# A fused mixer and mixture-of-experts block: x squared on two engines, z in column groups, other release points for loads, expert 0 picked apart, last weights by columns

## What is computed

```python
h = rms_norm(x, norm_mix)
(cb, cc, cx, aq, ak, av, gq, gk, gv, gr, gz) = split(h @ w_in)     # gz: 16 columns, z
y_conv = short_conv(cb, cc, cx, conv_w, conv_b)
y_attn = moba_attention(rms_norm(aq), rms_norm(ak), av, rel_bias_table)
y_gla  = gla(gq, gk, gv, gr, gz, w_gla_alpha, ...)                 # uses gz @ w_gla_alpha
merged = sum_n sigmoid(h @ w_merge_gate[n]) * (y_n @ w_branch[n])
x  = x + merged @ w_out
h2 = rms_norm(x, norm_ffn)
x  = x + hier_moe(h2, ...)   # group by argmax of 4, then the top 2 of its 8 experts, weights from softmax;
                             # y = sum over the two chosen e: w * ((silu(h2 @ w_g[e]) * (h2 @ w_u[e])) @ w_d[e])
```

## Time and profile before

| | before |
|---|---|
| time of the runs, median (lowest to highest) | 712.26 us (711.34 to 715.14), 3 runs |
| profiled execution: time, span | 712.9 us, 711.1 us |
| PE busy | 587.2 us, 83% |
| DVE, ACT, POOL busy | 302.8, 189.7, 29.6 us |
| DMA moved | 247.73 MB, mean 348 GB/s |
| granted TensorE clock, mean | 0.894 |

### The profile page before, as it was taken

One profiled execution on the slowest core, in us unless ns is written; L12 is line 12 of the kernel. 1 busy time (PEld: TensorE's weight loads), 2 busy tenths in 40 slices (PEclk: granted clock), 3 DMA queues, 4 the chain that ended last, 5 costly groups with the idle time before them and its releaser, 6 DMA issues.

```text
span 711.1 us, 15452 instructions
## 1 busy us (share of the span) xinstructions
PE 587.2 (83%) x6636; PEld 410.9 (58%) x6636; DVE 302.8 (43%) x626; ACT 189.7 (27%) x332; POOL 29.6 (4%) x56
## 2 busy tenths in 40 slices
PE   8999999999999999996875767776678656887584
PEld 5787899999999885553432333333334333443342
DVE  6475976985474945442222222122312222111412
ACT  4493355473535434110111001010011100110111
POOL 8003000000000020000000000000000000000000
PEclk9999999999999999998798788797877988687969
DMA  8995546536579699999999999999999999999993
GB/s 253 349 328 187 163 137 203 175 121 213 175 274 420 234 395 369 427 425 428 425 427 425 426 429 427 426 427 427 425 425 428 427 427 427 424 426 427 423 417 146
DMA packets 39619, 247.73 MB, mean 348 GB/s; under 512 B 4360, under 2 KB 6496, under 8 KB 25472
## 3 DMA queue, kind: packets, MB, share of 16 engines
q1 hardware_dynamic: 38096, 245.44, 85.6%
q0 software_dynamic: 912, 1.25, 1.0%
q10 hardware_dynamic: 544, 0.06, 0.1%
HBM read 245.67 MB, written 1.06 MB: 347 GB/s over the span
## 4 chain that ended last, share of the span: by engine, by line
PE 50%; DMA 44%; SPq 1%; another core or an unknown queue 1%; DVE 1%; issue 1%; ACT 0%; ACTq 0%; DVEq 0%
DMA wide<-in_w_expert_up 38%; PE ps L1366 8%; PE ps L1029 6%; PE ps L1030 6%; PE ps L1031 6%; DMA wide<-in_w_expert_down 3%; PE ps L1401 3%; PE ps L1002 3%; PE ps L1004 3%; PE ps L1003 3%; PE ps L1325 2%; DMA ring<-in_w_in 2%; PE ps L1413 1%; PE ps L1381 1%; SPq L526 1%
## 5 line engine op out<-in xcount | busy, mean ns | idle before, releaser
L1366 PE MATMUL ps<-wide,xe 128*32 128x256 f32 x2048 | 162.1, 470 | 109.3 <-DMA wide<-in_w_expert_up 109.3
L1366 PEld LDWEIGHTS ps<-wide,xe 128*32 128x32 f32 x2048 | 75.9, 131 | 176.9 <-issue 132.1
L1882 DVE TENSOR_TENSOR xe<-ps,g_ffn 128x256 f32<-128x256 f32 x32 | 13.6, 425 | 258.4 <-PE ps L1334 258.4
L1486 DVE TENSOR_TENSOR ring_lo<-ring,w_hi 128x1024 fp32r<-128x1024 f32 x76 | 92.0, 1228 | 46.2 <-ACT w_hi L721 45.7
L721 ACT ACTIVATE w_hi<-ring 128x1024 fp32r<-128x1024 f32 x76 | 79.0, 1058 | 58.8 <-PE ps L1031 35.3
L1029 PE MATMUL ps<-hT_hi,w_hi 128*128 128x256 f32 x320 | 89.4, 279 | 0.2 <-DVE hT_lo L1498 0.2
L1030 PE MATMUL ps<-hT_lo,w_hi 128*128 128x256 f32 x320 | 88.4, 276 | 0.0
L1031 PE MATMUL ps<-hT_hi,ring_lo 128*128 128x256 f32 x320 | 88.4, 276 | 0.0
L925 ACT ACTIVATE he<-ps 128x128 f32<-128x128 f32 x32 | 8.9, 278 | 207.7 <-PE ps L1381 204.7
L1401 PE MATMUL ps<-wide,he 128*32 128x256 f32 x1024 | 62.5, 382 | 1.9 <-DMA wide<-in_w_expert_down 1.8
L1029 PEld LDWEIGHTS ps<-hT_hi,w_hi 128*128 128x128 f32 x320 | 60.1, 188 | 0.7 <-issue 0.7
(11 more groups left out here) (276 smaller groups left out, 785.9 us busy)
## 6 DMA issues: line engine op xcount, KB each, us to landing
wide<-in_w_expert_gate SPq DMA_DIRECT2D x27, 2048.0 KB, 45.6
wide<-in_w_expert_up SPq DMA_DIRECT2D x27, 2048.0 KB, 48.2
wide<-in_w_expert_down SPq DMA_DIRECT2D x27, 2048.0 KB, 41.1
ring<-in_w_in SPq DMA_DIRECT2D x8, 2048.0 KB, 16.1
ring<-in_w_merge_gate SPq DMA_DIRECT2D x6, 2048.0 KB, 9.6
wide<-in_w_expert_gate SPq DMA_DIRECT2D x10, 1024.0 KB, 13.2
wide<-in_w_expert_up SPq DMA_DIRECT2D x10, 1024.0 KB, 10.6
wide<-in_w_expert_down SPq DMA_DIRECT2D x9, 1024.0 KB, 11.8
```

The lines of the kernel that those rows point to most:

```text
L1366: ins = t_.matmul(ps[q * WIN:(q + 1) * WIN, b, 0:QW], xe[b][:, k % 2, k // 2, :], w, start=(k == 0), stop=(k == KD - 1))
L1486: v.tensor_tensor(piece(ring_lo, g, c), piece(ring, g, c), by_row(out_hi[g == 19][c]).bitcast(F32), ALU.subtract).then_inc(wpre_lo, 1)
```

## The change

1. Front. Tile 1 of x is squared and summed by ACT; roots and reciprocals are taken for each tile by itself; DVE multiplies in four halves (features k 0 to 3 of both tiles, then 4 to 7), and PE turns each half when it is there. 14 warm-up matmuls for 20. Group 1 no longer waits for the small loads; w_z is loaded by ACT's queue; w_al is loaded four times, by SP behind group 1 (after two new memsets of POOL); POOL's 15 small loads wait for group 1.
2. z. 16 fp32 matmuls without hi and lo, slice k into the column group k mod 4, so that four parts of z lie in 128 partitions; w_al's four copies sum them in the next matmul.
3. w_out. New events after the halves of out_half and after the matmuls of out_quarter(1, q) that read ring_lo, which come first now. They release 12 and 14, 16, and 17.
4. Routing. in_group(0) and best_two(0) stand before x1_add(1, 2). Expert 0's own places come from six small matmuls on a mask `first`; the 14 `spots`, slots, table and pass count follow behind rows_in(0, 0). Seeds are single quarters in other places. SP issues units 22 to 25 before it reads the number of passes.
5. Tail. The last unit comes in column pieces of 512, 256 and 256; down, ACT's copy and combine of expert 31 run piece by piece in fp32 without y_lo, DVE makes all final copies, and SP stores six blocks.

The diff, cut to its core:

```diff
-N_WARM = 20
+N_AHEAD = 4
+N_WARM = 14
+LAST = (slice(0, 2 * QW), slice(2 * QW, 3 * QW), slice(3 * QW, D))
+LAST_Q = ((0, 1), (2,), (3,))
@@ SP
-                elif n < 16:
+                elif n in (12, 14):
+                    sp.wait_ge(chunk_done, chunks_before[NPRE - 2] + 1)
+                elif n in (13, 15):
                     sp.wait_ge(proj_done, first_bank[NPRE - 2] + 2)
-                elif n in (16, 18):
+                elif n == 16:
+                    sp.wait_ge(chunk_done, chunks_before[NPRE - 2] + 2)
+                elif n == 18:
                     sp.wait_ge(proj_done, first_bank[NPRE - 2] + 4)
+                elif n == 17:
+                    sp.wait_ge(chunk_done, chunks_before[NPRE - 2] + 3)
...
+                    if g == 1:
+                        sp.wait_ge(sbd_zero, 1)
+                        for q in range(NQ):
+                            sp.dma_start(w_al[WIN * q:WIN * q + 16, :], w_gla_alpha[0]).then_inc(alpha_in, 16)
...
-                    sp.wait_ge(early_in, 16 * N_EARLY)
-                    sp.dma_start(w_z[:, :, :], w_in_v[:, :, 4608:4624]).then_inc(wz_in, 16)
...
+            for n in range(RING, RING + N_AHEAD):
+                next_load(n, 0)
             sp.wait_ge(route_ready, 1)
@@ POOL
+            g.memset(w_z[:, :, 16:WIN], 0.0)
+            g.memset(w_al[:, :], 0.0).then_inc(sbd_zero, 1)
...
+            pool.wait_ge(landed[1], 16)
             for dst, src in smalls:
@@ ACT
-            act.wait_ge(ms_ready, 2)
-            s_.activation(stat[:, 2:4], stat[:, 0:2], ACT.Sqrt).then_inc(rms_ready, 1)
+            act.wait_ge(x_in[1], 16)
+            s_.activation(xn[:, 1, :], x_tok[:, 1, :], ACT.Square, accum_out=stat[:, 1:2]).then_inc(x_sq, 1)
+            for tt in range(TT):
+                act.wait_ge(ms_ready, tt + 1)
+                s_.activation(stat[:, 2 + tt:3 + tt], stat[:, 6 + tt:7 + tt], ACT.Sqrt).then_inc(rms_ready, 1)
...
+            def y_last(p):
...
+                for i, qs in enumerate(LAST_Q):
...
+                    s_.activation(y_end[rows_i, :], ps[rows_i, 0, 0:QW], ACT.Copy,
+                                  scale=w_slot[rows_i, ...]).then_inc(y_last_ready, 1)
@@ PE, z
-                t_.matmul(o, w_z_hi[:, k, :], hT_hi[:, k, :], start=(k == 0), stop=False)
-                t_.matmul(o, w_z_hi[:, k, :], hT_lo[:, k, :], start=False, stop=False)
-                ins = t_.matmul(o, w_z_lo[:, k, :], hT_hi[:, k, :], start=False, stop=(k == KD - 1))
+            for j in range(KD // NQ):
+                for h in (hT_hi, hT_lo):
+                    for q in range(NQ):
+                        ins = t_.matmul(ps[WIN * q:WIN * (q + 1), 4, 0:T], w_z[:, k, :], h[:, k, :].bitcast(F32), ...)
@@ PE, w_out and routing
+                if tt and ks[0] == 0:
+                    for k in range(KD):
+                        ins = t_.matmul(o, merged_hi[:, k, rows], wl[k], start=(k == 0), stop=False)
+                    ins.then_inc(chunk_done, 1)
...
-            out_quarter(1, 1, range(0, 4))
+            out_quarter(1, 1, range(0, 2))
...
-            out_quarter(1, 1, range(4, 6))
+            out_quarter(1, 1, range(2, 6))
...
+            seed(0, 0)
             route(1, range(6, KD), 6)
-            seed(0, 0)
+            seed(0, 2)
+            seed(1, 0)
+            seed(1, 2)
             seed(0, 1)
+            seed(0, 3)
...
+            for k in range(TOPK):
+                first_spot(tri_bf[:, :], 0, k, 0, start=(k == 0), stop=False)
+                first_spot(ones_bf[:, :], 0, k, 1, start=False, stop=False)
+                ins = first_spot(tri_bf[:, :], 1, k, 1, start=False, stop=(k == TOPK - 1))
             ins.then_inc(pos_mm, 1)
+            seed(1, 1)
...
             pick_rows(0, 0)
+            seed(1, 3).then_inc(seeded, 1)
             turn_rows(0, 0)
-            seed(1, 1).then_inc(seeded, 1)
+            all_spots()
@@ PE, tail
+            def down_last(p):
...
+                    for j in range(2):
+                        for q in qs:
+                            ins = t_.matmul(ps[q * WIN:(q + 1) * WIN, 0, 0:QW], he[:, 2 + j, :], ...)
...
+                    if i:
+                        combine_last(p, i - 1)
+                combine_last(p, 2)
@@ DVE
-            norm_stats(x_tok, [xn[:, tt, :] for tt in range(TT)], ms_ready)
-            norm_apply(x_tok, xn, rms_ready, xn_ready)
+            norm_stats(0)
+            norm_stats(1)
+            norm_apply(0, range(0, 4))
+            norm_apply(1, range(0, 4))
+            norm_apply(0, range(4, KD))
+            norm_apply(1, range(4, KD))
...
             group_of(0)
+            in_group(0)
+            best_two(0)
             x1_add(1, 2)
             square_sum(1, 2)
             mean_square(1)
-            in_group(0)
             scale_out(1)
-            best_two(0)
             group_of(1)
...
+            rows_in(0, 0)
+            slots()
             dve.wait_ge(table_ready, 1)
             choose(0, 1)
-            rows_in(0, 0)
```

More of the change, by code:

```diff
@@ L184, in hybrid_block @@
         le = place("le", [P, TT, NE], F32)
+        first = place("first", [P, TT, TOPK], BF16)
         eh = place("eh", [P, TT, TOPK, NE], BF16)
@@ L240, in hybrid_block @@
         scr = here("scr", [P, 2, C], F32)
+        w_z = place("w_z", [P, KD, WIN], F32, at=scr_at)
         la, e_pos, e_neg, e_rest = (qTz[:, 2 * i:2 * i + 2, :] for i in range(4))
@@ L582, in _ @@
                         load_unit(n)
[L583 to L594, removed]
+                    for n in range(RING, RING + N_AHEAD):
+                        next_load(n, UNITS * p)
+                for n in range(RING + N_AHEAD, UNITS):
+                    next_load(n, UNITS * p)
+            for i, cols_i in enumerate(LAST):
+                for tt in range(TT):
+                    sp.wait_ge(fin_ready, 2 * i + tt + 1)
+                    sp.dma_start(out[0, tt * P:(tt + 1) * P, cols_i], fin[tt][:, cols_i]).then_inc(stored, 16)
+            sp.wait_ge(stored, 16 * TT * len(LAST))
         @block.gpsimd
@@ L777, in _ @@
                 s_.activation(scr[:, tt, :], bank(4 if tt == 0 else 7), ACT.Square).then_inc(o_sq, 1)
-            act.wait_ge(o_ms, 1)
-            s_.activation(stat[:, 16:24], stat[:, 8:16], ACT.Sqrt).then_inc(o_rms, 1)
+            act.wait_ge(head_ms, 1)
+            s_.activation(stat[:, 16:24], stat[:, 8:16], ACT.Sqrt).then_inc(head_rms, 1)
             act.wait_ge(small_in, 16 * N_SMALL)
@@ L787, in _ @@
             high_pre(5, (1, 2, 3))
-            act.wait_ge(qk_ms, 1)
-            s_.activation(qkr[:, :, :, :], qkm[:, :, :, :], ACT.Sqrt).then_inc(qk_rms, 1)
+            act.wait_ge(head_ms, 2)
+            s_.activation(qkr[:, :, :, :], qkm[:, :, :, :], ACT.Sqrt).then_inc(head_rms, 1)
             high_pre(6, (0, 1, 2))
@@ L909, in _ @@
             rows_copy(0, 0)
+            act.wait_ge(slot_ready, 1)
+            s_.activation(flat(tab[:, :, :]), ps[:, 3, 2 * NE:4 * NE], ACT.Copy).then_inc(table_ready, 1)
             passes = act.alloc_register("passes_act")
@@ L954, in _ @@
                 y_high(p, NE - 2)
-                y_high(p, NE - 1)
-            for tt in range(TT):
-                act.wait_ge(combined, turns * (4 * NE) + 8)
-                s_.activation(fin[tt][:, 0:C].rearrange("p (q n) -> p q n", q=2), ps[:, 4:6, QW * tt:QW * (tt + 1)], ACT.Copy).then_inc(fin_act, 1)
+                y_last(p)
         @block.tensor
@@ L1230, in out_quarter @@
                     wh = out_hi[1][c][:, QW * (k % 4):QW * (k % 4 + 1)]
[L1231 to L1233 removed]
+                    t_.matmul(o, merged_hi[:, k, rows], wh, start=(tt == 0 and k == 0), stop=False)
+                    if tt == 0:
+                        t_.matmul(o, merged_hi[:, k, rows], wl[k], start=False, stop=False)
                     ins = t_.matmul(o, merged_lo[:, k, rows], wh, start=False, stop=(k == KD - 1))
@@ L1243, in turn_x1, with seed @@
                 ins.then_inc(x1_turned, 1)
-            def seed(tt, half):
-                for q in (2 * half, 2 * half + 1):
-                    ins = t_.matmul(bank(4 + q, 2)[:, tt, :], ident[:, :], x_tok[:, tt, QW * q:QW * (q + 1)],
-                                    start=(tt == 0), stop=False, skip_group_check=True)
-                return ins
+            def seed(tt, q):
+                return t_.matmul(bank(4 + q, 2)[:, tt, :], ident[:, :], x_tok[:, tt, QW * q:QW * (q + 1)],
+                                 start=(tt == 0), stop=False, skip_group_check=True)
             def route(tt, ks, copied):
```

253 lines of the change are left out of this document (148 added, 105 removed).

## The result

| | before | after |
|---|---|---|
| time of the runs, median (lowest to highest) | 712.57 us (711.34 to 715.14), 4 runs | 722.14 us (719.00 to 723.03), 4 runs |
| profiled execution: time, span | 712.9, 711.1 us | 721.93, 720.1 us |
| PE, DVE, ACT, POOL busy | 587.2, 302.8, 189.7, 29.6 us | 592.1, 302.5, 192.6, 29.5 us |
| granted TensorE clock, mean | 0.894 | 0.900 |

The changed kernel is slower by 1.2%: ratio 1.0123, 95% interval 1.0101 to 1.0145. I had forecast 711.3 with 708.4 to 715.0 around it, so it lies 7.1 us above the range. PE is busy 4.9 us longer though it does hardly any other work and its mean clock is no lower, which already says that a wait alone can't be the cause.

A forecast was written before the change was run, and what follows sets the result against it. PE bounds the kernel to about 262 us, DMA from about 280, routing between. Front -0.45, routing with N_AHEAD -0.5 and tail 0 sum to -0.95: 711.9 profiled, 711.3 as median, range 708.4 to 715.0.

The forecast's parts named there:

- Front, x: Start of the kernel, path of x to the first projection matmul: about 12.7 us instead of 11.66, +1.0 (+0.4 to +2.1).
- the step on the small loads: Front: POOL's 15 small loads and the bias store behind them wait for group 1; first users come much later: nothing.
- Front, z and group 1: Front: z takes 1.9 us instead of 2.75, -0.85, and the wait for group 1's first piece goes, -0.6.
- Rival (a), one table: Front, ACT: one table serves Square and Sqrt, roots 1.28 us earlier, front -1.7, time 710.0; chance 0.12.
- Rival (c), the clock: Front, PE: pauses after warm-up let the clock fall, feat(0) at half speed, +2.7 us; 714.0 to 715.9; chance 0.17.
- w_out's events: w_out stage: units 12, 14, 16 and 17 are issued earlier, but unit 22 still waits for gate_up: nothing.
- rival (b): Weight stream: holes in slices 14 to 16 count as lost bytes and come back, time 706 to 707; chance 0.09.
- Routing: Router to expert 0: x1_add(1, 2) moves by 0.94 us, mostly given back; gate_up(0) +0.1 (-0.5 to +0.6).
- N_AHEAD: SP's loads behind gate_up(0): unit 22 no longer waits for the pass count, -0.8 us, of which about 0.6 counts.
- Tail: End of the kernel, last PE matmuls to stores: later last store, smaller stores, net 0 us (-0.8 to +0.8).

The follow-up runs named there:

- experiment 1: The changed kernel with b_al's load raising alpha_in again instead of gain_in: 716.90 us, ratio 1.0076 to the kernel before.
- 128-byte kernel: The changed kernel with b_al off gain_in and 96 bytes left free behind `first`, making the shift 128 bytes: 718.04 us beside 711.65.
- experiment 3: Changed kernel, b_al off gain_in, shift 128 bytes: 718.04 us; with Sqrt first 716.02; the two kernels named: old w_out waits 717.45, N_AHEAD 0 719.12.
- experiment 2: Changed kernel shifted 64 bytes: 721.62 us; also with b_al off gain_in: 716.50; kernel before with 32 bytes ahead of eh: 718.23, 5.9 from placement.

## Why the prediction was wrong, step by step

The sum had no term for two things, and they are the whole loss of 9.6: the wait for b_al (5.2 by the medians of experiment 1, 3.9 in the trace), and the shift by `first` (716.90 to 711.65, 5.3 by the medians, 5.4 in the trace). With both mended the change gives 711.65 beside 712.21: 0.56 less, where the sum had 0.95 less; the interval of that ratio, 0.9978 to 1.0011, holds both this and no gain at all. One by one:

- **Front, x**: right without the wait for b_al, +1.0: 12.63 for 12.7, halves of 0.49 and 0.43 for 0.5, and two table loads as the earlier trace rows suggested. In the changed kernel itself it is +3.4. What failed is the step on the small loads: I counted the loads that ACT's queue and POOL's issue, but not who waits for them. A semaphore that is shared by two loads waits for the later one, and w_z's descriptors had just been put ahead of it.
- **Front, z and group 1**: right. z takes 1.86 (28.64 to 30.50) for the 1.9 forecast, and group 1 waits for nothing.
- **Rival (a), one table**: didn't happen, since the Square comes first. With a Sqrt first it does: 1.6 us earlier roots for the 1.28 that I had priced, and 2.0 and 0.9 at the end in two pairs of kernels. The Trainium skill (ScalarE activation tables: per-element evaluation and per-set limits, section Table sets in the compiler and the runtime) says that the compiler's back end places the loads per block, by the greedy longest run. The two loads of the changed kernel (at 3.72 and 7.41), though one table serves both functions, disagree, unless the two stand in different blocks, which no run shows.
- **Rival (c), the clock**: its mechanism ran, with another cause and less than its price: 1.52 us in feat(0) for 2.7, behind a pause of 2.96. Behind the 0.59 ahead of feat(0) that is left without b_al it did not run. But I had all pauses below 1 us, and that was wrong: between warm-up and transposes it is 2.16 in the changed kernel and 0 to 2.24 in the others, and in the 128-byte kernel the clock fell behind 1.81 of it. The table matmul then came at 25.31 instead of 23.70 to 24.01 in the two kernels named in experiment 3, so (c) can happen as I described it, in some executions and at about 1.5 us.
- **w_out's events**: right, nothing; rival (b) is out.
- **Routing**: right where the clock held: in the changed kernel w_out to gate_up(0) takes 35.91, +0.13 for +0.1. In the eight profiles in which it fell it is +1.5 to +1.7. In the profiled execution this is no part of the loss. I priced the later x1_add at 0.94 of time, and not what a wait of 1.41 does to the clock, having taken 2.11 in the earlier trace rows as harmless.
- **N_AHEAD**: unit 22 goes 2.02 behind gate_up(0) instead of 2.80, as forecast. Without N_AHEAD (experiment 3) it is 4.55, since the number of passes now comes later; unit 26 is issued 12.2 behind gate_up(0) either way. What of it reaches the end isn't settled.
- **Tail**: right, 0. From the first matmuls of the last unit's column pieces to the end 9.05 us pass (711.01 to 720.06), from those of the earlier trace rows 9.07.
- **The tiles**: the step that failed most. The list of `place` calls is part of the whole diff, and I gave it no cost because no instruction changes. The trace of before couldn't have priced it, and what stands behind it is counted only now: some 1150 feature matmuls (960 with hT, 192 with ya and yg) and 240 of 512 columns; 4.5 ns and 3 to 4 ns on each are 5.2 and 0.8, together 6.0 for the 5.9 of experiment 2.

The row of the first of these matmuls in section 5 of the page (count, busy us, mean ns, idle before), of before and then of after, holds both causes, the slower mean and the wait:

```profile
L1029 PE MATMUL ps<-hT_hi,w_hi 128*128 128x256 f32 x320 | 89.4, 279 | 0.2 <-DVE hT_lo L1498 0.2
```
```profile
L1055 PE MATMUL ps<-hT_hi,w_hi 128*128 128x256 f32 x320 | 91.6, 286 | 3.0 <-DVE hT_lo L1587 3.0
```

## What to carry to other kernels

When a load changes its semaphore, or a count in a wait goes up, list every load that now raises it and where each stands in its queue, before anything is costed. A new tile is an edit too: lay it behind the others, or compare the addresses of all tiles that PE reads. When an operation gets slower by the same few ns everywhere, with no wait and at full clock, look first whether its data has moved, as it had here. A wait that one puts on PE is to be priced twice, as time and as clock: work under the lower clock right behind it may be what the next stage waits for. And one profile shows one execution: the same wait of 1.41 us brought the clock down in eight kernels and not in three.

## What the runs showed of the hardware

- The pace of fp32r matmuls of 256 columns depends on the distance between the rows that stream and the weights: 113, 117.5 or 120 ns apart at distances of 192, 224 or 64, and 0 mod 256 bytes, up to 6%. When both move together by 64 bytes, or the distance grows by 256, nothing changes. The Trainium skill (TensorE: Matmul & The Clock Gate, section Step-by-step: what each phase is for) says that loading the next weights takes no read bandwidth from the running matmul. By that alone the distance would make no difference; here it makes up to 6%. Why it does, no run shows.
- The distance that is best for one form isn't for the other: 0 is the worst of the four for feat (120 ns) and no worse than any other for tok (227 for 226 to 232 at a distance of 192).
- The granted clock fell to 0.50 (1.2 GHz) behind waits of PE of 1.41 us in eight of eleven profiles, and held at 1.00 in the other three with the same wait; it held behind 0.44 and 0.59. It fell behind 1.81 in the front of one kernel and held behind 2.24 in that of another. A pause can't be called harmless from one row, as I did with 2.11.
- ACT's small load of b_al took 9.6 us to land behind w_z's 1024 descriptors (in the kernel with b_al off gain_in), and 7.3 in the kernel before, where w_z was in SP's queue. In the first case group 1's load also starts 6.6 us earlier; the two aren't separated.
